# Head norms of the recurrence as two fp32r products on split squares, each step one slot later

## The chip, the core and the metric

The kernel runs on one core of one Trainium2 chip, in one launch. The metric is the device time of that launch in microseconds (us). The core has TensorE (PE: matmuls; its weight loads are shown apart, as PEld), VectorE (DVE), ScalarE (ACT), GpSimd (POOL), and the queues that issue transfers. Each engine works through its own instructions in the order in which they were written; semaphores are the only tie between engines. A wait therefore holds up everything that stands behind the waiting instruction on its engine.

## What is computed

A trunk of two layers on 512 tokens of width 1024. Each layer is a half step of a SwiGLU network, a mixer of three kinds of heads in parallel, a second half step, and a gated embedding:

```
x = x + 0.5 * swiglu(rms_norm(x, ffn1_norm[i]), ...)
x = x + hybrid_mixer(rms_norm(x, mix_norm[i]), i, w_in[i], w_out[i], ...)
x = x + 0.5 * swiglu(rms_norm(x, ffn2_norm[i]), ...)
gate = jax.nn.sigmoid(rms_norm(x, ple_norm[i]) @ ple_w_gate[i])
x = x + gate * rms_norm(p[i] @ ple_w_proj[i], ple_post_norm[i])
```

The mixer projects x once and cuts the result into tiles. Queries and keys of the attention heads, and the output of the recurrence, are normed per head of 64 (or 32) values:

```
q_n = rms_norm(nq.reshape(b, t, NSA_HEADS, HEAD_DIM), nsa_q_norm)
k_s = rms_norm(kvh(sk), nsa_k_norm[1]);  k_w = rms_norm(kvh(wk), nsa_k_norm[2])
k_d = rms_norm(dk.reshape(b, t, DIFF_HEADS, 2, DIFF_QK_DIM), diff_k_norm)
o_h = hgrn2_scan(q_h, i_gate, hi..., log_f)
o_h = rms_norm(o_h, hgrn_out_norm) * jax.nn.silu(hg...)
```

The recurrence (`hgrn2_scan`) is computed as a causal product with decays. The kernel builds its scores level by level, for blocks that double in size.

## The kernel before

Values lie with their features across the 128 partitions and the 512 tokens along the free side. A large product is made from split operands: each fp32 array is kept as a high part rounded to fp32r and an fp32r remainder, and `three` (L531 to L533) issues high by high, low by high and high by low. PE takes an fp32r matmul as one instruction, and an fp32 matmul as two.

**The recurrence** runs between the first projections (`group_c`) and the attention. It has 30 slots: three pairs of heads p, and for each the levels -1 to 8, so slot = 10 p + lev + 1. In what follows level product s is PE's product of slot s. All engines loop over the same slots, each in its own order:

- PE (`hgrn`, L728): the level's score products (L676) into two of the four `side` banks; in slots 10 and 20 also `hgrn_values(p - 1)` (L689, L696), which gathers the output of the pair before; then filler for the dense array: products of the projection of `natA` (slots 0 to 7) or of the tiles nq0, nq1, nq2, sk, wk, dk0, dk1 (`tile_part`, from slot 9 on, two or three of a tile's eight parts in a slot).
- ACT (L1213, L1227, L1230): the exponential of the decays for the level two slots on; in slots p, lev = 7 and 8 it also copies far scores out of the banks (`far_scores`, L1243), for which `hgrn_values` waits; it rounds the weights of the chunk two places on to their high part (`split`, L1048).
- POOL (L497): the two operands `zv` of a level, from ACT's decays, in two buffers.
- DVE: the exponents for the level two slots on (L1816, L1818), then `keep` (L1833 or L1839), which copies the level's scores out of its two banks and so frees them; evacuation of a finished tile (`scaled`, L1716); the low part of a weight chunk (L1580).

**A head norm** is four steps on a [128, 512] tile. ACT squares it into one of two buffers (`head_square`, L1086, `sq`). PE multiplies by a block matrix of ones (`head_squares`, L566), in fp32, into a `side` bank. ACT turns that into the factor with Ln and Exp (`head_factor`, L1097 and L1100), after which the bank is free. DVE multiplies (`normed`, L1736, or for the recurrence's output `out_norm`, L1881). In the recurrence of each layer eight norms are made so: of the pairs 0 and 1 of the recurrence's output, ("hgrn", 0) and ("hgrn", 1), and of nq0, nq1, nq2, sk, wk, dk0. For a tile whose last product part stands in slot t, the square stands in slot t + 1, the ones product at the end of slot t + 2, factor and multiplication in slot t + 3 (`tiles_after`). Six more head norms of a layer, and the compressed keys', stand elsewhere.

The `side` banks are handed out in turn. A level takes two, a ones product one, and the taker waits until the former content of its bank is read.

## Time and profile before

| what | value |
|---|---|
| median of 3 runs | 2235.11 us (2234.0 to 2235.28) |
| the profiled execution | 2234.47 us, of which 2232.7 us are its span from first to last instruction |
| granted TensorE clock | 0.999 of full |
| busy: PE, DVE, ACT, POOL | 2217.7, 1184.8, 916.4, 154.9 us |
| recurrence, layer 0 / layer 1 | from 445 to 555 us / from 1554 to 1664 us of the span |

Times in the rows below count from the start of the span. A row of a timeline is a start, a duration, the engine, the line, the operation, the names out<-in, the shape and how many instructions are merged in it. In brackets stands idle time of the engine just before it and who ended it. A matmul's shown duration reaches beyond the start of the next, since they are pipelined; what a matmul costs is the distance from start to start. The same holds, by some 0.08 us, for DVE and ACT.

### The profile page before, as it was taken

The page shows a single profiled execution, that of the slowest core. Times are in us where ns is not written, and L with a number is a line of the kernel's source. Part 1 is how long each engine was busy: PE and PEld are TensorE (multiplying, and loading weights), DVE is VectorE, ACT ScalarE, POOL GpSimd, SP SyncE. Part 2 cuts the span into 40 slices and gives each one's busy share as a digit, 9 for nine tenths or more (in the row PEclk, how much of TensorE's full clock was granted, in tenths as well). Part 3 has the DMA queues.
Part 4 walks back from the last instruction along what each step waited for, and adds up shares of the span by engine and source line. Part 5 has one row for each costly group of instructions (what it writes and reads, how often), then busy time and mean ns, then how long its engine had stood idle before and what let it go on. Part 6 is the DMA issues. An engine that isn't in the chain of part 4 may idle for free. (4 is left out here: it accounts for less than half of the span.)

```text
span 2232.7 us, 29159 instructions
## 1 busy us (share of the span) xinstructions
PE 2217.7 (99%) x11564; PEld 1755.3 (79%) x11564; DVE 1184.8 (53%) x1934; ACT 916.4 (41%) x1518; POOL 154.9 (7%) x155
## 2 busy tenths in 40 slices
PE   9999999999999999999999999999999999999999
PEld 7888888876667888888888888878766678888887
DVE  6444433577785444433664443346776764444336
ACT  5222223545784322222552222235557752232234
POOL 0000000033111000000000000000431210000000
PEclk9999999999999999999999999999999999999999
DMA  6323334312113323333222333343121132333332
GB/s 207 127 95 103 89 96 143 131 58 77 55 37 90 104 95 97 100 103 100 95 95 95 101 97 91 100 150 117 58 75 48 43 102 95 99 100 101 96 98 83
DMA packets 69280, 214.40 MB, mean 96 GB/s; under 512 B 8175, under 2 KB 15343, under 8 KB 69146
## 3 DMA queue, kind: packets, MB, share of 16 engines
q1 hardware_dynamic: 60452, 191.10, 27.2%
q10 hardware_dynamic: 8694, 21.45, 2.9%
q8 instruction: 92, 1.51, 0.3%
q14 instruction: 42, 0.34, 0.0%
HBM read 208.30 MB, written 5.40 MB: 96 GB/s over the span
## 5 line engine op out<-in xcount | busy, mean ns | idle before, releaser
L531 PE MATMUL main<-xh,wh 128*128 128x512 f32 x1896 | 756.0, 399 | 3.7 <-DVE wl L2130 2.0
L533 PE MATMUL main<-xh,wl 128*128 128x512 f32 x1896 | 740.4, 391 | 0.0
L532 PE MATMUL main<-xl,wh 128*128 128x512 f32 x1896 | 740.4, 390 | 0.0
L1580 DVE TENSOR_TENSOR wl<-raw,wh 128x1024 fp32r<-128x1024 f32 (+2 forms) x336 | 404.3, 1204 | 354.9 <-ACT wh L1048 353.6
L1048 ACT ACTIVATE wh<-raw 128x1024 fp32r<-128x1024 f32 (+1 forms) x370 | 375.4, 1016 | 452.2 <-PE main L533 425.0
L531 PEld LDWEIGHTS main<-xh,wh 128*128 128x128 f32 x1896 | 356.6, 188 | 101.0 <-issue 21.8
L533 PEld LDWEIGHTS main<-xh,wl 128*128 128x128 f32 x1896 | 356.6, 188 | 75.2
L532 PEld LDWEIGHTS main<-xl,wh 128*128 128x128 f32 x1896 | 356.7, 188 | 74.3 <-issue 3.8
L532 PE MATMUL main<-ffl,wh 128*128 128x512 f32 x704 | 274.3, 390 | 0.0
L531 PE MATMUL main<-ffh,wh 128*128 128x512 f32 x704 | 274.3, 390 | 0.0
L533 PE MATMUL main<-ffh,wl 128*128 128x512 f32 x704 | 274.3, 390 | 0.0
L1112 ACT ACTIVATE fg<-fg 128x512 f32<-128x512 f32 x88 | 55.6, 632 | 398.4 <-DVE fg L1672 398.4
L1672 DVE TENSOR_TENSOR fg<-main,rb 128x512 f32<-128x512 f32 x88 | 60.8, 691 | 235.0 <-PE main L533 218.2
L532 PEld LDWEIGHTS main<-ffl,wh 128*128 128x128 f32 x704 | 132.3, 188 | 27.4
L533 PEld LDWEIGHTS main<-ffh,wl 128*128 128x128 f32 x704 | 132.3, 188 | 27.3
L531 PEld LDWEIGHTS main<-ffh,wh 128*128 128x128 f32 x704 | 132.2, 188 | 27.3
L1685 DVE TENSOR_TENSOR fu<-main,rb 128x512 f32<-128x512 f32 x88 | 60.8, 690 | 147.2 <-PE main L533 147.2
L497 POOL TENSOR_TENSOR zv<-ev,hall 128x256 f32<-128x256 f32 x108 | 82.0, 782 | 258.5 <-ACT ev L1213 200.1
L1381 ACT ACTIVATE probs<-probs,small 128x128 f32<-128x128 f32 (+3 forms) x160 | 87.5, 551 | 1.7 <-DVE small L1987 1.7
L506 POOL TENSOR_TENSOR wl<-raw,wh 128x768 fp32r<-128x768 f32 (+1 forms) x34 | 69.0, 2036 | 235.7 <-ACT wh L1048 235.7
L478 POOL MEMSET w2p<- 128x768 f32 x2 | 1.5, 740 | 1153.6 <-PE main L533 1153.6
L1839 DVE COPY_PREDICATED sdiag<-lmask,side 128x512 f32<-128x512 uint32 x84 | 57.1, 733 | 17.0 <-PE side L676 17.0
(262 smaller groups left out, 2082.4 us busy)
## 6 DMA issues: line engine op xcount, KB each, us to landing
raw<-in_ffn_gate SPq DMA_DIRECT2D x87, 512.0 KB, 3.5
raw<-in_ffn_up SPq DMA_DIRECT2D x87, 512.0 KB, 3.4
raw<-in_ffn_down SPq DMA_DIRECT2D x64, 448.0 KB, 3.3
raw<-in_w_in_t SPq DMA_DIRECT2D x40, 512.0 KB, 3.5
raw<-in_ffn_down SPq DMA_DIRECT2D x32, 512.0 KB, 3.6
raw<-in_wout SPq DMA_DIRECT2D x24, 384.0 KB, 3.2
w<-in_cmp_w ACTq DMA_DIRECT2D x16, 512.0 KB, 4.3
raw<-in_ple_gate SPq DMA_DIRECT2D x16, 512.0 KB, 3.3
```

What stands on the lines that cost most here:

```text
L497: nc.gpsimd.tensor_tensor(o.rearrange(cut, two=2, l=size)[:, :, which, :], e.rearrange(cut, two=2, l=size)[:, :, which, :], operand.rearra ...
L506: nc.gpsimd.tensor_tensor(wl[:, c % SLOTS, 0:n], raw[:, c % SLOTS, 0:n], wh[:, c % SLOTS, 0:n], ALU.subtract).then_inc(*tick("weights_lo_p ...
L531: nc.tensor.matmul(out, lh, rh, start=start, stop=False, **kw)
L532: nc.tensor.matmul(out, lh, rl, start=False, stop=False, **kw)
L533: return nc.tensor.matmul(out, ll, rh, start=False, stop=stop, **kw)
L1048: nc.scalar.activation(wh[:, c % SLOTS, 0:n], raw[:, c % SLOTS, 0:n], ACT.Copy).then_inc(*tick("weights_hi", c, layer="all"))
L1112: nc.scalar.activation(fg[:, ft % 2, :], fg[:, ft % 2, :], ACT.Silu).then_inc(*tick("gate_silu", name, ft))
L1381: nc.scalar.activation(pr, pr, ACT.Exp, bias=sm("nm", k), scale=-1.0, accum_out=sm("sum", k)).then_inc(*tick("probs", u, g, i))
L1580: nc.vector.tensor_tensor(wl[:, c % SLOTS, 0:n], raw[:, c % SLOTS, 0:n], wh[:, c % SLOTS, 0:n], ALU.subtract).then_inc(*tick("weights_lo", ...
L1672: nc.vector.tensor_tensor(fg[:, ft % 2, :], bank_of((name + "_gate", ft))[:], rb[:], ALU.mult).then_inc(*tick("gate_scaled", name, ft, fre ...
L1685: nc.vector.tensor_tensor(fu[:, ft % 2, :], bank_of((name + "_up", ft))[:], rb[:], ALU.mult).then_inc(*tick("up_scaled", name, ft, frees=( ...
L1839: ins = V.copy_predicated(out, m, src)
```

## The change

Eight norms of each layer's recurrence are changed, 16 in all. ACT squares the tile twice: in fp32 into `zs[:, 0]`, and rounded to fp32r into `zhi`. DVE subtracts (`square_low`) and writes the fp32r remainder `zlo`. PE multiplies an fp32r copy of the block matrix with `zhi` and then with `zlo`, two one-instruction matmuls instead of a two-instruction one. `zhi`, `zlo` and buffer 0 have no second copy, so a square of such a norm, and the one after it, wait for the ones product of the norm just before. (`zhi` and `zlo` lie where two arrays of the attention or of the network are not in use at the time.)

The steps stand in slots by two tables: the square at `SQUARED_AT`, the subtraction one slot later, the ones product two slots later and now right behind the level's products (and behind `hgrn_values`), ahead of the tile parts; Ln, Exp and the multiplication at `FACTOR_AT`. ACT's Ln and Exp now stand behind `far_scores`, where they stood ahead. The multiplication of a recurrence output moves from lev 1 to lev 2.

```diff
+SQUARED_AT = {("hgrn", 0): 10, "nq0": 12, "nq1": 15, "nq2": 18, ("hgrn", 1): 20, "sk": 22, "wk": 24, "dk0": 27}
+FACTOR_AT = {("hgrn", 0): 13, "nq0": 15, "nq1": 18, "nq2": 21, ("hgrn", 1): 23, "sk": 25, "wk": 27, "dk0": 29}
...
@@ PE, head_squares @@
+                    if name not in SQUARED_AT:
+                        pe.wait_ge(*done("head_sq", name))
+                        nc.tensor.matmul(out[:, 0:n], const_(blocks), zs[:, slot_of(name) % 2, 0:n], start=True,
+                                         stop=True).then_inc(*tick("head_squares", name))
+                        return
+                    pe.wait_ge(*done("blocks_rounded", 1, layer=0))
+                    pe.wait_ge(*done("head_sq_lo", name))
+                    nc.tensor.matmul(out[:], blocks_r[blocks][:], zhi[:], start=True, stop=False)
+                    nc.tensor.matmul(out[:], blocks_r[blocks][:], zlo[:], start=False,
                                      stop=True).then_inc(*tick("head_squares", name))
...
@@ PE, hgrn @@
-                        if p and lev == 0:
-                            head_squares(("hgrn", p - 1), "sum64")
+                        for name in named_at(SQUARED_AT, slot - 2):
+                            head_squares(name, "sum32" if name[0] == "d" else "sum64")
...
-                        for name in tiles_after(slot, 2):
-                            head_squares(name, "sum32" if name[0] == "d" else "sum64")
...
@@ ACT, head_square @@
-                    if k >= 2:
+                    if k >= 1 and (name in SQUARED_AT or norm_order[k - 1] in SQUARED_AT):
+                        act.wait_ge(*done("head_squares", norm_order[k - 1]))
+                    elif k >= 2:
                         act.wait_ge(*done("head_squares", norm_order[k - 2]))
...
+                    if name in SQUARED_AT:
+                        nc.scalar.activation(zs[:, 0, :], operand, ACT.Square).then_inc(*tick("head_sq", name))
+                        nc.scalar.activation(zhi[:], operand, ACT.Square).then_inc(*tick("head_sq_hi", name))
+                        return
...
@@ DVE, hgrn @@
-                            if p and lev == 1:
+                            if p and lev == 2:
                                 out_norm(("hgrn", p - 1), 4 + p, col("hout"), "hgrn_out", p - 1)
...
-                            for name in tiles_after(slot, 3):
-                                normed(name)
+                            for name in named_at(SQUARED_AT, slot - 1):
+                                square_low(name)
+                            for name in named_at(FACTOR_AT, slot):
+                                if name in NORMED:
+                                    normed(name)
...
+                def square_low(name):
+                    dve.wait_ge(*done("head_sq_hi", name))
+                    nc.vector.tensor_tensor(zlo[:], zs[:, 0, :], zhi[:],
+                                            ALU.subtract).then_inc(*tick("head_sq_lo", name))
```

Two copies on DVE in the first network make the fp32r block matrices, once.

PE, slots 13 and 14 (levels 2 and 3 of the second pair of heads). `zv` are a level's operands; L676 becomes L697, L566 becomes L586 and L587, L531 to L533 become L545 to L547. Before:

```order
L676 MATMUL side<-zv 64x64 [waits head_ln,near_scores,decayed]
L676 MATMUL side<-zv 64x64 x15
...
L533 MATMUL main<-xh,wl 128x512
L566 MATMUL side<-sq,const 128x512 [waits head_sq,near_scores]
L676 MATMUL side<-zv 64x64 [waits near_scores,decayed]
L676 MATMUL side<-zv 64x64 x15
L531 MATMUL main<-xh,wh 128x512
```

After, slot 14 and the head of slot 15:

```order
L697 MATMUL side<-zv 64x64 [waits head_ln,near_scores,decayed]
L697 MATMUL side<-zv 64x64 x15
L586 MATMUL side<-zhi,sum_r 128x512 [waits head_sq_lo,blocks_rounded,near_scores]
L587 MATMUL side<-zlo,sum_r 128x512
L545 MATMUL main<-xh,wh 128x512
...
L697 MATMUL side<-zv 64x64 [waits near_scores,decayed]
```

The ones product of nq0 moved from the end of slot 13, ahead of level product 14, to behind it, and it waits for DVE's subtraction instead of ACT's square.

DVE, from `keep` of slot 12 to that of slot 14. Before:

```order
L1839 COPY_PREDICATED sdiag<-lmask,side 128x512 [waits masks_in,near_scores,hgrn_scores] x2
L1881 SCALAR_TENSOR_TENSOR mixed<-main,cols,acc 128x512 [waits head_factor]
L1716 TENSOR_TENSOR z<-main,rb 128x512 [waits product]
L1580 TENSOR_TENSOR wl<-raw,wh 128x1024 [waits weights_hi]
L1816 TENSOR_TENSOR ev<-hall 128x16x16 [waits decayed]
L1818 TENSOR_TENSOR ev<-hall 128x16x16
L1839 COPY_PREDICATED sdiag<-lmask,side 128x512 [waits masks_in,near_scores,hgrn_scores] x2
L1816 TENSOR_TENSOR ev<-hall 128x8x32 [waits decayed]
L1818 TENSOR_TENSOR ev<-hall 128x8x32
L1839 COPY_PREDICATED sdiag<-lmask,side 128x512 [waits masks_in,near_scores,hgrn_scores] x2
```

After, the same stretch:

```order
L1865 COPY_PREDICATED sdiag<-lmask,side 128x512 [waits masks_in,near_scores,hgrn_scores] x2
L1742 TENSOR_TENSOR z<-main,rb 128x512 [waits product]
L1604 TENSOR_TENSOR wl<-raw,wh 128x1024 [waits weights_hi]
L1842 TENSOR_TENSOR ev<-hall 128x16x16 [waits decayed]
L1844 TENSOR_TENSOR ev<-hall 128x16x16
L1865 COPY_PREDICATED sdiag<-lmask,side 128x512 [waits masks_in,near_scores,hgrn_scores] x2
L1916 SCALAR_TENSOR_TENSOR mixed<-main,cols,acc 128x512 [waits head_factor]
L1910 TENSOR_TENSOR zlo<-sq,zhi 128x512 [waits head_sq_hi]
L1842 TENSOR_TENSOR ev<-hall 128x8x32 [waits decayed]
L1844 TENSOR_TENSOR ev<-hall 128x8x32
L1865 COPY_PREDICATED sdiag<-lmask,side 128x512 [waits masks_in,near_scores,hgrn_scores] x2
```

The output norm's multiplication (L1881, now L1916) moved behind the `keep` of slot 13, and the subtraction for nq0 (L1910) stands behind it.

ACT, slot 18 (level 7 of the second pair), from the decay's exponential to that of slot 19. Before:

```order
L1213 ACTIVATE ev<-ev 128x512 [waits exponent]
L1243 ACTIVATE soff<-side 128x128 [waits hgrn_values,hgrn_scores]
...
L1048 ACTIVATE wh<-raw 128x1024 [waits product,raw_full2]
L1086 ACTIVATE sq<-z 128x512 [waits head_squares,scaled]
L1213 ACTIVATE ev<-ev 128x512 [waits exponent]
L1243 ACTIVATE soff<-side 128x256 [waits hgrn_values,hgrn_scores]
```

After:

```order
L1238 ACTIVATE ev<-ev 128x512 [waits exponent]
L1268 ACTIVATE soff<-side 128x128 [waits hgrn_values,hgrn_scores]
...
L1122 ACTIVATE acc<-side,const 128x512 [waits hgrn_out,head_squares]
L1125 ACTIVATE acc<-acc 128x512 [waits head_ln]
L1067 ACTIVATE wh<-raw 128x1024 [waits product,raw_full2]
L1108 ACTIVATE sq<-z 128x512 [waits head_squares,scaled]
L1109 ACTIVATE zhi<-z 128x512
L1238 ACTIVATE ev<-ev 128x512 [waits exponent]
L1268 ACTIVATE soff<-side 128x256 [waits hgrn_values,hgrn_scores]
```

Ln and Exp of nq1 came into slot 18 from slot 17, behind the far scores and ahead of the rounding of the weights, and a second square follows.

## Rows read from the trace of the kernel before

**Rows 1.** The page: busy us, share of the span, instructions of each engine.

```profile
PE 2217.7 (99%) x11564; PEld 1755.3 (79%) x11564; DVE 1184.8 (53%) x1934; ACT 916.4 (41%) x1518; POOL 154.9 (7%) x155
```

**Rows 2.** PE's waits: us in total, times, longest.

```profile
PE side L843 <- ACT soff L1243: 0.7, 1, 0.7
PE side L676 <- DVE sdiag L1839: 0.5, 2, 0.3
```

**Rows 3.** Busy time by engine in one stretch, slots 15 to 17.

```profile
core 0: us, PE busy (x) PEld busy (x) DVE busy (x) ACT busy (x) POOL busy (x), PEclk, DMA share, GB/s
497.61:506.54 8.93, 8.91 (x107) 6.35 (x107) 8.16 (x13) 6.00 (x14) 5.04 (x8) 1.00 0.20 61
```

**Rows 4.** PE's timeline, layer 0, slot 11 and slots 13 to 14.

```profile
484.66 0.69 PE L676 MATMUL side<-zv 64*64 64x64 f32 x32
485.29 1.13 PE L566 MATMUL side<-sq,const 128*128 128x512 f32 x2
...
486.49 0.40 PE L532 MATMUL main<-xl,wh 128*128 128x512 f32 x1
486.72 0.40 PE L533 MATMUL main<-xh,wl 128*128 128x512 f32 x1
...
493.22 0.39 PE L533 MATMUL main<-xh,wl 128*128 128x512 f32 x1
493.45 1.02 PE L566 MATMUL side<-sq,const 128*128 128x512 f32 x2
494.40 0.69 PE L676 MATMUL side<-zv 64*64 64x64 f32 x32
```

**Rows 5.** DVE, a subtraction that writes fp32r: group by form, busy us, mean ns.

```profile
L1678 DVE TENSOR_TENSOR ffl<-fu,ffh 128x512 fp32r<-128x512 f32 x88 | 60.1, 683 | 0.4
```

**Rows 6.** DVE's timeline, slots 12 to 14, 16 and 18.

```profile
489.18 1.38 DVE L1839 COPY_PREDICATED sdiag<-lmask,side 128x512 f32<-128x512 uint32 x2 [1.58 <-PE side L676]
490.45 0.73 DVE L1881 SCALAR_TENSOR_TENSOR mixed<-main,cols,acc 128x512 f32<-128x512 f32 x1
491.10 0.68 DVE L1716 TENSOR_TENSOR z<-main,rb 128x512 f32<-128x512 f32 x1
491.70 1.22 DVE L1580 TENSOR_TENSOR wl<-raw,wh 128x1024 fp32r<-128x1024 f32 x1
492.83 0.42 DVE L1816 TENSOR_TENSOR ev<-hall 128x256 f32<-128x256 f32 x1
...
493.50 1.35 DVE L1839 COPY_PREDICATED sdiag<-lmask,side 128x512 f32<-128x512 uint32 x2
...
498.16 0.78 DVE L1736 SCALAR_TENSOR_TENSOR q<-z,small,rn 128x512 f32<-128x512 f32 x1 [0.67 <-ACT rn L1100]
...
502.80 1.34 DVE L1839 COPY_PREDICATED sdiag<-lmask,side 128x512 f32<-128x512 uint32 x2
...
509.52 1.23 DVE L1580 TENSOR_TENSOR wl<-raw,wh 128x1024 fp32r<-128x1024 f32 x1 [1.71 <-ACT wh L1048]
```

**Rows 7.** PE's timeline: level products 15, 17, 18, then values; 15 of layer 1.

```profile
497.61 0.70 PE L676 MATMUL side<-zv 64*64 64x64 f32 x32 [0.25 <-DVE sdiag L1839]
...
503.66 0.68 PE L676 MATMUL side<-zv 64*64 64x64 f32 x16
506.54 0.72 PE L676 MATMUL side<-zv 64*128 64x128 f32 x8
...
514.04 0.44 PE L689 MATMUL main<-sdiag,hv 128*64 128x128 f32 x4
...
1606.34 0.69 PE L676 MATMUL side<-zv 64*64 64x64 f32 x32 [0.26 <-DVE sdiag L1839]
```

**Rows 8.** ACT's timeline, slots 14 and 19.

```profile
496.26 0.63 ACT L1213 ACTIVATE ev<-ev 128x512 f32<-128x512 f32 x1 [2.01 <-DVE ev L1818]
...
511.99 1.19 ACT L1243 ACTIVATE soff<-side 128x256 f32<-128x256 f32 x4
```

**Rows 9.** One DVE line: duration ns least, median, most.

```profile
L1818 DVE TENSOR_TENSOR ev<-hall x42: 409/417/958, 435.9 to 1644.4; 128x256 f32<-128x256 f32 x42
```

More of the change, by code:

```diff
@@ L61 @@
 SMALL = {}
-for _name, _n in (("gq", 1), ("gdq", 1), ("gsub", 1), ("nlam", 1), ("lam2", 64), ("e", 8),
+for _name, _n in (("gq", 1), ("gdq", 1), ("gsub", 1), ("nlam", 1), ("e", 8),
                   ("max", 3), ("tot", 3), ("rec", 3), ("lb", 6), ("lc", 6), ("li", 6), ("ab", 6), ("rt", 4),
@@ L67 @@
 NSMALL = _at
+SMALL["lam2"] = (SMALL["cmax"][0], 64)
 TILES = ["ck", "cv", "hf0", "hf1", "hf2", "hq0", "hq1", "hq2", "sk", "wk", "nq0", "nq1", "nq2", "dk0", "dk1", "dq0",
@@ L100, with named_at @@
 PARTS, LAST_PART = slot_parts()
+SQUARED_AT = {("hgrn", 0): 10, "nq0": 12, "nq1": 15, "nq2": 18, ("hgrn", 1): 20, "sk": 22, "wk": 24, "dk0": 27}
+FACTOR_AT = {("hgrn", 0): 13, "nq0": 15, "nq1": 18, "nq2": 21, ("hgrn", 1): 23, "sk": 25, "wk": 27, "dk0": 29}
+def named_at(places, slot):
+    return [name for name in places if places[name] == slot]
 def tiles_after(slot, distance):
@@ L253, in layers @@
         sq = sb("sq", [P, 2, SEQ])
+        sq_at = place["at"] - 4 * 2 * SEQ
+        zlo = nc.alloc_sbuf_tensor_at("zlo", [P, SEQ], F32R, offset=sq_at)
+        zhi = nc.alloc_sbuf_tensor_at("zhi", [P, SEQ], F32R, offset=sq_at + 4 * SEQ)
+        blocks_r = {name: sb(name + "_r", [P, P], F32R) for name in ("sum64", "sum32")}
         region = place["at"]
@@ L564, in head_squares @@
                     out = take(("head_squares", name), which)
-                    pe.wait_ge(*done("head_sq", name))
-                    nc.tensor.matmul(out[:, 0:n], const_(blocks), zs[:, slot_of(name) % 2, 0:n], start=True,
+                    if name not in SQUARED_AT:
[7 more added lines that the diff above has]
+                    nc.tensor.matmul(out[:], blocks_r[blocks][:], zlo[:], start=False,
                                      stop=True).then_inc(*tick("head_squares", name))
@@ L1283, in hgrn @@
                                     split(CHUNK[(name,)] + AHEAD)
-                            for name in tiles_after(slot, 1):
-                                act.wait_ge(*done("scaled", name))
-                                head_square(name, zt(name))
+                            for name in named_at(SQUARED_AT, slot):
+                                if name in NORMED:
+                                    act.wait_ge(*done("scaled", name))
+                                    head_square(name, zt(name))
                             if (p, lev) == (2, 1):
@@ L1620, in small_exponents @@
                                         ALU.add).then_inc(*tick("fold"))
+                        for n, name in enumerate(("sum64", "sum32")):
+                            V.tensor_copy(blocks_r[name][:], const_(name)).then_inc(*tick("blocks_rounded", n))
                     dve.wait_ge(params_in[counts.layer], 32)
```

7 lines of the change are left out of this document (3 added, 4 removed).

## The prediction

> **What bounds the kernel now.** The page first: PE is busy 2217.7 us of a span of 2232.7 [rows 1], so what makes PE's queue shorter is a gain unless it makes PE wait. Then PE's own waits: in the recurrence they are few and short, 0.25 us in each layer for DVE's `keep` before level product 15, and 0.67 us in layer 0 for ACT's far scores before the first attention scores [rows 2, 7]. Then the stretches, for how close the others are. In slots 15 to 17 DVE is busy 8.16 us of 8.93 [rows 3]. DVE has half of the whole span free [rows 1], but hardly a tenth here, in the place where the change gives it more to do. Last the timelines of PE, DVE and ACT over slots 11 to 19, on which the sum rests. Layer 1 repeats layer 0 some 1108.7 us later (level product 15 at 497.61 and 1606.34, with the same wait [rows 7]), so I work out layer 0 and take it twice, but for the 0.67, which only layer 0 has.
>
> **What is removed on PE.** An fp32 ones product occupies PE for 0.95 us from its start to the next level product (493.45 to 494.40), or 0.86 us where an fp32r product follows: the first ones product starts at 485.29, the second instruction of the following triple at 486.49, and that is 0.34 after the triple's first [rows 4]. (0.34 is what a triple's first takes behind fp32 work; the further ones take 0.23, 486.49 to 486.72.) The two fp32r matmuls that replace it take 0.23 each and inherit the 0.34 of the change of type from the tile part behind them: 0.46 more in the queue. The gain is 0.86 - 0.46 = 0.40 us for each norm, 8 x 0.40 = 3.2 a layer. With the two old waits, if they go (0.25 and 0.67), and some 0.2 of gaps around the old instructions, that is 4.3 us in layer 0.
>
> **What is added.** On ACT a second square of 0.6 us, on DVE a subtraction. The nearest row of that form, two fp32 operands in SBUF and an fp32r result, takes 683 ns [rows 5], about 0.60 from start to start. ACT's is hidden in most slots. DVE's is what PE now waits for, and PE's queue is short of slack towards it: the ones product stands one slot after the subtraction, right behind the level product, and all of PE's work of the slot stands behind it. The two rounded copies of the ones matrices are 128x128 and in the first network, where DVE waits for PE most of the time: nothing.
>
> **The walk, slots 12 to 14.** Level product 12 comes 0.86 earlier, since the ones product of slot 11 is gone, and so does the `keep` that waits for it: 488.32 instead of 489.18 [rows 6]. Then in DVE's new order, by start-to-start distances of the same rows: keep 1.27, tile evacuation 0.60, weights 1.13, exponents 0.67, keep 1.24, which ends at 493.23. Here stands the multiplication for ("hgrn", 0), which needs ACT's decay, Ln and Exp. In slot 14 of before these three took from 496.26 until DVE went on at 498.16, 1.90 [rows 6, 8]. In the new slot 13 they start when the exponents are there, at 492.12, so DVE idles until 494.03. Then 0.65 for the multiplication and 0.65 for the subtraction of nq0: `zlo` is there at 495.36. PE meanwhile: level product 14 stood at 494.40; less 0.86 and 0.95, plus 0.46, it could start at 493.1. Its bank wants the Ln of ("hgrn", 0), done at 493.3: 0.2 lost. It is through at 494.0, and the ones product waits until 495.4: 1.4 lost. **Slot 14 costs 1.6 us**, and level product 15 starts at 498.1, half a microsecond later than before.
>
> **Slot 17.** Before, the `keep` of slot 16 ran from 502.80 [rows 6], when PE was almost at level product 17 (503.66 [rows 7]): DVE is a slot behind. In the new order it has two subtractions more in front of or behind that `keep`, the multiplication of nq0 ahead of it, and the head start of 0.86. I get 504.8 for the `zlo` of nq1, PE through level product 17 at 503.8: **1.0 lost**. Level product 18 starts at 507.6 instead of 506.54.
>
> **Slots 18 to 20.** ACT's far scores of slot 19, for which `hgrn_values(1)` waits, started at 511.99 [rows 8], last in a chain: far scores of slot 18, rounded weights (ACT), their low part (DVE, at 509.52 after idling 1.71 for ACT [rows 6]), exponents (DVE), decay (ACT). Before, that ended 0.9 ahead of the values at 514.04 [rows 7]. Now Ln and Exp of nq1 stand inside it (0.70 + 0.54), then the multiplication of nq1 ahead of the exponents (0.73), and the chain starts 0.5 later with level product 18. So the far scores end at 515.7 and PE is there at 514.2: **1.5 lost**.
>
> **Slots 20 to 29**, counted from the end of the values, since DVE's `keep` of slot 20 waits for them. Up to the subtraction of ("hgrn", 1) DVE has keep, exponents, keep (which waits for level product 21, 3.3 after the values' end), evacuation, weights and subtraction: ready at 7.1 after. PE, with the ones product of nq2, the three parts of sk, level product 21, three parts of wk and level product 22, gets there at 5.5: **1.6 lost**. sk, wk and dk0 find their `zlo` ready. But level product 25 wants the `keep` of slot 24, which stands behind DVE's scores of the compressed keys (**0.5**), and level product 26 wants the Ln of sk, behind ACT's second square of wk (**0.65**). The far scores of slot 29, now ahead of dk0's Ln and Exp, come early enough for the first attention scores. DVE enters the attention some 3.5 late, PE 2.5; I take no further stall there, since DVE has waits for PE in its first logits.
>
> Sum of a layer: 1.6 + 1.0 + 1.5 + 1.6 + 0.5 + 0.65 = 6.85 lost, 4.3 gained: +2.5 in layer 0, and without the 0.67 +3.2 in layer 1: +5.7. The 2234.47 of the profiled execution (2232.7 of span and 1.8 around it) become 2240.2. The median of the runs stands 0.64 above the profiled one: **2240.8 us**.
>
> **A rule of the Trainium skill against the change.** One exponent instruction of DVE took 958 ns at most where the median of its line is 417 [rows 9]. The skill ("SBUF — State Buffer", "SBUF: two separate sides") says that GpSimd and a DVE instruction with two SBUF inputs take one pair of ports in turn, whole instruction by whole instruction; the trace's 958 fits it, since that line reads two SBUF operands too. The subtraction has two such inputs. What this would do is a rival of its own, priced from the same row.
>
> **Rivals.**
> - *The cover holds* (faster). DVE and ACT keep up, no ones product waits. For it: ACT is busy 6.00 of 8.93, and the table gives every step a slot. Against it: rows 3 and the idle 0.67 at 498.16, which shows DVE bound by ACT's latency. It gives 2235.1 - 4.3 - 3.6 = 2227.2. Chance 0.13.
> - *Half of it* (same). The ones products wait, but the two chains that I carried furthest, values(1) and the pair of level products 25 and 26, come out even: 2 x (1.5 + 1.15) = 5.3 less, 2235.5. The error of a walk grows with its length, and DVE may catch up by some 1 us in its idle times (1.71 at 509.52). Chance 0.26.
> - *The walk* (slower by 0.25%). It needs no mishap, only the orders and durations of before. Chance 0.46, own range 2238 to 2243.5.
> - *Ports* (slower). Each subtraction in the path (nq0, nq1, ("hgrn", 1)) meets POOL and takes 0.54 more (958 - 417), six in two layers, 3.2: 2244.0. It decides from the first of them that overlaps a product of POOL. Chance 0.12.
> - *The two fp32r matmuls cost what the fp32 one did*: then 2 x 3.2 more, 2247.2. Against it is every triple in rows 4. Chance 0.03.
>
> **Numbers.** Likeliest 2240.8. The low end leaves out the cover that holds, the high end takes in the ports with an error of 2: 2231 to 2246. A measurement of this kernel tells about 0.2% (4.5 us) from no change. Faster than 2230.6: 0.15, the cover and a little of the second. Above 2239.6: some 0.33 of the walk's 0.46 and the last two (0.15): 0.48. Between: 0.37.
>
> **What would show it.** Right: in the new profile the ones product (L586) waits for DVE's `zlo`, over 1 us, in slots 14, 17 and 22 of both layers, and L710 (values) waits for `soff` in slot 20; the level products of slots 15 and 18 start some 0.5 and 1 us later than 497.61 and 506.54. A norm's two fp32r matmuls take 0.46. Wrong: if `zlo` of nq0 is ready by 494.0, the first term falls, and with it the sum, since all later ones start from there.

## The result, and the profile after

| | before | after |
|---|---|---|
| median (range, runs) | 2235.12 us (2233.84 to 2235.28, 6) | 2251.57 us (2250.66 to 2252.49, 6) |
| the profiled span | 2232.7 us | 2250.7 us |

The ratio of the times is 1.0075 (95% interval 1.0065 to 1.0086): slower by 0.75%. The prediction had the sign, slower, but its 2240.8 is 10.8 us short and its range ended at 2246.

PE is busy for as long as in [rows 1], and the span is 18.0 longer. That the two busy times are equal is chance: the cheaper products shorten PE's work, and a lower clock, further down, lengthens it again (in the first experiment, where the clock stays up, PE is busy 2213.3 us). From the page of after, the busy line:

```profile
PE 2217.7 (99%) x11564; PEld 1758.0 (78%) x11564; DVE 1200.0 (53%) x1952; ACT 924.7 (41%) x1534; POOL 158.3 (7%) x155
```

PE's waits of after, over the whole span (us in total, times, longest). Where [rows 2] had 1.2 us in three waits, the lines of the recurrence now hold 19.5:

```profile
PE side L586 <- DVE zlo L1910: 13.8, 8, 2.8
PE main L710 <- ACT soff L1268: 2.9, 2, 1.5
PE side L697 <- DVE sdiag L1865: 1.8, 4, 0.6
...
PE side L697 <- ACT rn L1122: 1.0, 2, 0.5
```

Now PE's timeline of after in layer 0, at the places of [rows 7] and of the prediction's steps (start, duration, line, operands; in brackets the idle time ahead and who ended it):

```profile
495.57 0.47 PE L586 MATMUL side<-zhi,sum_r 128*128 128x512 f32 x1 [1.35 <-DVE zlo L1910]
...
498.27 0.69 PE L697 MATMUL side<-zv 64*64 64x64 f32 x32
...
505.81 0.47 PE L586 MATMUL side<-zhi,sum_r 128*128 128x512 f32 x1 [1.75 <-DVE zlo L1910]
...
508.52 0.72 PE L697 MATMUL side<-zv 64*128 64x128 f32 x8
...
516.73 0.44 PE L710 MATMUL main<-sdiag,hv 128*64 128x128 f32 x4 [1.47 <-ACT soff L1268]
...
526.33 0.47 PE L586 MATMUL side<-zhi,sum_r 128*128 128x512 f32 x1 [1.64 <-DVE zlo L1910]
...
549.21 1.14 PE L697 MATMUL side<-zv 64*128 64x256 f32 x8
552.88 0.76 PE L586 MATMUL side<-zhi,sum_r 128*128 128x512 f32 x1 [2.54 <-DVE zlo L1910]
...
555.28 1.65 PE L862 MATMUL side<-kk,q 64*128 64x128 f32 x8
...
559.46 0.92 PE L862 MATMUL side<-kk,q 64*128 64x384 f32 x4
```

The same two places in the trace of before (level product 29, second attention scores), and the wait for the subtraction of dk0 in layer 1 of after:

```profile
545.33 1.14 PE L676 MATMUL side<-zv 64*128 64x256 f32 x8
...
550.47 0.92 PE L843 MATMUL side<-kk,q 64*128 64x384 f32 x4
```

```profile
1671.35 0.47 PE L586 MATMUL side<-zhi,sum_r 128*128 128x512 f32 x1 [2.83 <-DVE zlo L1910]
```

The waits of slots 14, 17, 20 and 22 are those of the prediction, that of slot 17 longer. The one at 552.88, for the subtraction of dk0 in slot 29, is not: there the prediction had none. Level product 29 stood at 545.33 before, so 549.21 is 3.9 late; the second attention scores stood at 550.47, so 559.46 is 9.0 late. More is lost in the ten microseconds after level product 29 than in the eighteen slots ahead of it. Layer 1 adds 9.1 in the same way.

What holds DVE there, from its timeline of after (its line L1762 is the multiplication of a norm, L2002 the three small products of the compressed keys) and POOL's:

```profile
546.76 0.68 DVE L1742 TENSOR_TENSOR z<-main,rb 128x512 f32<-128x512 f32 x1
547.35 2.63 DVE L1762 SCALAR_TENSOR_TENSOR kk<-z,cols,acc 128x512 f32<-128x512 f32 x1
549.90 2.83 DVE L1910 TENSOR_TENSOR zlo<-sq,zhi 128x512 fp32r<-128x512 f32 x1
...
553.97 0.34 DVE L2002 TENSOR_TENSOR small<-small,gates 128x8 f32<-128x8 f32 x3
```

```profile
547.04 5.15 POOL L520 TENSOR_TENSOR wl<-raw,wh 128x1024 fp32r<-128x1024 f32 x2
```

The two DVE instructions, 0.75 and 0.68 us elsewhere, take 5.38 us together, about as long as GpSimd's two products beside them (5.15). In both kernels GpSimd starts these products right behind level product 28. In the kernel before, DVE was a slot further on by then: it had the multiplication behind it and no subtraction to do, and it was the three tiny instructions of 8 elements that took 3.20 us, with nobody waiting for them. From the trace of before, POOL and DVE:

```profile
542.30 4.71 POOL L506 TENSOR_TENSOR wl<-raw,wh 128x1024 fp32r<-128x1024 f32 x2
```

```profile
542.61 0.94 DVE L1962 TENSOR_REDUCE small<-cp 128x24 f32<-128x768 f32 x1
...
543.92 3.20 DVE L1967 TENSOR_TENSOR small<-small,gates 128x8 f32<-128x8 f32 x3
```

And what follows the stall: busy time and granted clock (PEclk) of after, in stretches around it and, last, in layer 1 behind the wait for the subtraction of nq0.

```profile
core 0: us, PE busy (x) PEld busy (x) DVE busy (x) ACT busy (x) POOL busy (x), PEclk, DMA share, GB/s
550.34:552.88 2.54, 0.01 (x1) 0.03 (x1) 2.54 (x2) 1.21 (x4) 1.85 (x1) 0.88 0.66 206
552.88:554.00 1.12, 1.12 (x3) 0.93 (x4) 1.05 (x3) 0.00 (x0) 0.00 (x0) 0.50 0.72 172
...
558.00:559.00 1.00, 1.00 (x4) 0.81 (x3) 0.28 (x2) 0.00 (x0) 0.00 (x0) 0.50 0.00 0
559.00:560.00 1.00, 1.00 (x6) 0.37 (x5) 0.00 (x0) 0.00 (x0) 0.00 (x0) 0.95 0.00 0
...
1614.00:1615.00 1.00, 1.00 (x3) 0.76 (x3) 1.00 (x3) 0.46 (x1) 0.47 (x1) 0.50 0.00 0
```

PE is granted 1.2 GHz instead of 2.4 for some 6.8 us at the stall of layer 0 (the last 0.6 us of the stall are among them), for 3.4 us behind that of layer 1, and for 3.4 us from 1613.8 on. At the lower clock the fp32r matmuls of a triple follow each other in 0.43 us instead of 0.23. In the trace of before the clock is at its full level from the 13th microsecond to the last three.

**The account.** The fp32 product of dk0 stood ahead of level product 29; its two fp32r matmuls, 0.46 us, now stand behind it. In layer 0, 3.9 to level product 29, these 0.46, 2.54 of stall, less the old wait of 0.67: 6.2. The second scores are 9.0 late, so the low clock took 2.8. In layer 1 level product 29 is 4.3 late (0.5 of it low clock, by the first experiment, where that layer has 3.8), then 0.46, 2.83 of stall and 1.6 of low clock: 9.1. So of some 18.1, the orders took 3.9 + 3.8 + 2 x 0.46 - 0.67 = 7.9, where the prediction had 5.7; the two stalls took 5.4 and the low clock 4.9, where it had nothing. The first experiment, with neither stall nor low clock, confirms the split: its second scores of layer 0 are 4.7 earlier than in after, which is 2.54 less a new wait of 0.60, and 2.8.

### The profile page after: what moved, and what is told of

Its sections match the earlier page's. It is cut to its first block and busy times, and to the rows that moved or that the text cites. A ratio compares the mean times of both kernels' runs of the same rounds, so it can differ in the third digit from the quotient of the medians.

```text
span 2250.7 us, 29195 instructions
## 1 busy us (share of the span) xinstructions
PE 2217.7 (99%) x11564; PEld 1758.0 (78%) x11564; DVE 1200.0 (53%) x1952; ACT 924.7 (41%) x1534; POOL 158.3 (7%) x155
## 5 line engine op out<-in xcount | busy, mean ns | idle before, releaser
L545 PE MATMUL main<-xh,wh 128*128 128x512 f32 x1896 | 753.9, 398 | 3.3 <-DVE wl L2165 1.6
L547 PE MATMUL main<-xh,wl 128*128 128x512 f32 x1896 | 740.6, 391 | 0.0
L545 PEld LDWEIGHTS main<-xh,wh 128*128 128x128 f32 x1896 | 357.0, 188 | 100.1 <-issue 20.5
L547 PEld LDWEIGHTS main<-xh,wl 128*128 128x128 f32 x1896 | 357.2, 188 | 76.0
L545 PE MATMUL main<-ffh,wh 128*128 128x512 f32 x704 | 273.9, 389 | 0.0
L547 PE MATMUL main<-ffh,wl 128*128 128x512 f32 x704 | 273.9, 389 | 0.0
L547 PEld LDWEIGHTS main<-ffh,wl 128*128 128x128 f32 x704 | 132.1, 188 | 27.6
L545 PEld LDWEIGHTS main<-ffh,wh 128*128 128x128 f32 x704 | 132.1, 188 | 27.3
```

Of the source, the lines that this page charges most:

```text
L545: nc.tensor.matmul(out, lh, rh, start=start, stop=False, **kw)
L547: return nc.tensor.matmul(out, ll, rh, start=False, stop=stop, **kw)
```

## Experiments

Times are medians. Those of the kernel before, which ran beside them, are 2234.68 for the first four, 2235.18 for the next four and 2234.78 for the last four; the differences below are to these. Starts of two traces are compared after taking off by how much they differ at slot 11, ahead of the change's first step (up to 1.3 us, from the start of the launch).

### GpSimd's product held back

```diff
 if own == layer and key in ON_GPSIMD:
     n = chunk_width(key)
+    if key == (GROUP_OF["B"][0],):
+        pool.wait_ge(*done("head_sq_lo", "dk0"))
```

> The changed kernel with one added wait: GpSimd's first product of the recurrence (the weights' first low half for the attention, 547.04 for 5.15 us in the trace of after) starts only when the subtraction of dk0 is done. Theory A (the missed term is slot 29: DVE's kk and subtraction of dk0 take 2.63 and 2.83 us beside that product, the ones product of dk0 waits 2.54 us, and the idle PE then gets the lower clock for some 7 us): kk and the subtraction take about 0.7 us each, the wait before the ones product of dk0 falls below 0.3 us, the granted clock behind it stays near 1.00, and the first attention scores start 4.5 to 5.5 us earlier in each layer: 2240 to 2243 us, close to the predicted walk. Rival B (the wait at slot 29 only uses up slack that is lost later anyway, since the attention's weights now come later from GpSimd): the wait goes, but a new one stands before the first attention tiles, and the time stays at 2249 to 2252. Rival C (the lower clock has another cause than the idle): the wait goes but the clock still falls: about 2246.

2243.24 us (2242.49 to 2243.76, 6 runs), 8.6 over before and 8 under after. DVE's and PE's timelines of this kernel, in layer 0:

```profile
548.02 0.74 DVE L1764 SCALAR_TENSOR_TENSOR kk<-z,cols,acc 128x512 f32<-128x512 f32 x1
549.32 0.69 DVE L1912 TENSOR_TENSOR zlo<-sq,zhi 128x512 fp32r<-128x512 f32 x1 [0.56 <-ACT zhi L1111]
```

```profile
550.95 0.50 PE L588 MATMUL side<-zhi,sum_r 128*128 128x512 f32 x1
...
552.98 0.93 PE L864 MATMUL side<-kk,q 64*128 64x128 f32 x8 [0.60 <-ACT rn L1124]
```

Both instructions are back at their length, the ones product of dk0 doesn't wait, and the clock behind it stays at 1.00. The first attention scores are 3.0 us earlier than in after in layer 0 and 4.0 in layer 1, where 4.5 to 5.5 was expected; the second ones, behind all of the low clock, are 4.7 and 4.9 earlier. **Theory A stands**, B and C fall for the larger part. The time is just above the expected range. Layer 0 has a new wait of 0.60: the attention scores want the bank that Ln of dk0 reads. So a little of B is in it. The waits of the other slots are what they were, but for one: that of nq1 in layer 1 is 1.75 here too, where after had 0.68. There the low stretch ahead of it delays level product 15 by 1.6 us, and DVE catches up meanwhile: of the 1.6 the shorter wait gives 1.1 back. GpSimd's product, pushed back, now stretches L2004, the three small products, to 3.61 us, again with nobody waiting.

### dk0 as before

The edit takes dk0 out of both tables and gives it the old steps:

```diff
+OLD_AT = {"dk0": 27}
 for name, ks in PARTS.get(slot, {}).items():
     tile_part(name, ks)
+for name in named_at(OLD_AT, slot - 1):
+    head_squares(name, "sum32" if name[0] == "d" else "sum64")
...
```

> The changed kernel with the last of the eight norms, dk0, as it was before: one square, one fp32 ones product at the end of slot 28, no subtraction. The other seven are as in the changed kernel. Theory A (slot 29 alone makes 5 to 6 us a layer): no wait of 2.5 us before a ones product in slot 29, no lower clock behind it, 0.4 us a layer lost on the fp32 product: 2240 to 2243 us. Rival B (kk, which GpSimd stretches too, delays the attention whatever the norm does): the gain is under 3 us, 2248 or more. Both earlier waits (ones products of slots 14, 17, 22, about 4.7 us a layer) stay.

2244.46 us (2243.93 to 2244.56, 4 runs), 9.8 over before. `kk` still takes 2.62 us beside GpSimd's product, but PE's next wait is the old one, 0.67 us for the far scores ([rows 2]), and the clock stays high. A stretched instruction costs only if PE waits for it: B falls. The time is 1.5 above the range of A. It is 1.2 slower than the first experiment: 0.4 for each of the two fp32 products is expected, and the rest is in their spread.

### TensorE doesn't wait for the subtraction

```diff
-pe.wait_ge(*done("head_sq_lo", name))
+pe.wait_ge(*done("head_sq_hi", name))
-nc.tensor.matmul(out[:], blocks_r[blocks][:], zlo[:], start=False,
+nc.tensor.matmul(out[:], blocks_r[blocks][:], zhi[:], start=False,
...
 act.wait_ge(*done("head_squares", norm_order[k - 1]))
+if norm_order[k - 1] in SQUARED_AT:
+    act.wait_ge(*done("head_sq_lo", norm_order[k - 1]))
```

> The changed kernel, but both fp32r matmuls of a norm read the rounded square, so TensorE doesn't wait for DVE's subtraction (the remainder is left out of the sum and the rounded square counted twice: the computation is changed). The subtraction is still done by DVE in its place, and ACT's next square waits for it too. Theory A (what costs is TensorE's wait for the subtraction): the waits of L586 (13.8 us in eight instructions in after) are nearly gone, the values' wait for the far scores stays in part, 2230 to 2238 us. Rival D (the added work on DVE and ACT costs through the other chains, the keep and far scores that come late, and the waits only move from the ones products to the level products): the waits of L586 go, but those for sdiag, rn and soff grow by as much, over 2243 us.

2241.76 us (2240.57 to 2242.14, 7 runs), 7.1 over before, between what the two theories expected. PE's waits of this kernel decide between them:

```profile
PE side L697 <- DVE sdiag L1867: 6.4, 8, 1.0
PE main L710 <- ACT soff L1270: 2.9, 2, 1.5
...
PE side L697 <- ACT rn L1124: 1.0, 2, 0.5
```

The 13.8 us before the ones products are gone, and the waits for `keep` (sdiag) have grown from 1.8 to 6.4. (ACT's added wait for the subtraction shows nowhere in this profile.) Of the 4.7 us of waits for `zlo` in slots 14, 17 and 22 of layer 0 little comes back: the values of slot 20 stand 1.1 us earlier than in after, level product 29 stands 1.2 earlier. Three quarters of what this trace gains over that of after are gained behind level product 29, and the first experiment has those without touching the other waits. **Theory A falls for slots 14 to 26, D holds there**: the waits for `zlo` are where DVE's lateness shows; take them away, and it shows one instruction later, at the level product.

### The fp32r pair alone, in the old slots

`PAIRED` are the eight norms, and `zr` are two fp32r buffers in the place of the two of `sq`.

```diff
-nc.scalar.activation(zs[:, k % 2, 0:n], operand, ACT.Square)
+to = zr[:, k % 2, :] if name in PAIRED else zs[:, k % 2, 0:n]
+nc.scalar.activation(to, operand, ACT.Square)
...
+if name in PAIRED:
+    half = zr[:, slot_of(name) % 2, :]
+    nc.tensor.matmul(out[:], blocks_r[blocks][:], half, start=True, stop=False)
+    nc.tensor.matmul(out[:], blocks_r[blocks][:], half, start=False, stop=True)
```

> The kernel before with two fp32r matmuls on a once rounded square in place of the fp32 ones product of the same eight norms, in the old slots, with no subtraction and no second square (the computation is changed: the remainder is left out and the rounded square counted twice). It measures the gain on TensorE by itself. By the prediction's term, 0.40 us for each of 16 norms: 2228 to 2230 us. Rival E (the pair costs what the fp32 product did): 2235. If the old waits go too (0.67 and 0.25), up to 1.2 us less.

2232.47 us (2232.04 to 2234.74, 10 runs), 2.2 under before (ratio 0.9990, interval 0.9981 to 1.0000). PE's timeline of this kernel in slot 11, to be laid beside [rows 4]:

```profile
485.03 0.50 PE L573 MATMUL side<-zr,sum_r 128*128 128x512 f32 x1
485.36 0.39 PE L574 MATMUL side<-zr,sum_r 128*128 128x512 f32 x1
485.59 0.39 PE L535 MATMUL main<-xh,wh 128*128 128x512 f32 x1
485.82 0.40 PE L536 MATMUL main<-xl,wh 128*128 128x512 f32 x1
```

From the ones product to the triple's second instruction it is 0.79 us, where [rows 4] have 1.20: 0.41 for one norm, the prediction's 0.40. But 16 of them bring 2.2 us and not 6.4. Of the missing 4.2, 2.0 stand in PE's keep waits (0.5 in [rows 2]), and some 0.8 in a gap ahead of the ones product of wk, of 0.6 in each layer, which the profile puts down to no other engine (in before it was under 0.2). The rest lies in gaps too short for this list:

```profile
PE side L687 <- DVE sdiag L1853: 2.5, 8, 0.4
...
PE side L573 <- issue: 1.1, 2, 0.6
```

**Even with nothing added on ACT or DVE the gain is a third of what the products give up.** Before, PE arrived at several level products just as DVE's `keep` freed their bank; there a faster PE only arrives early. The expected 2228 to 2230 is missed by 2.5 us.

### The move alone

One square, fp32 ones products, no subtraction, but all steps in the slots of the changed kernel:

```diff
-if name not in SQUARED_AT:
+if True:
     pe.wait_ge(*done("head_sq", name))
...
-for name in named_at(SQUARED_AT, slot - 1):
-    square_low(name)
```

> The norms' steps in the slots of the changed kernel (ones product right behind the level product two slots after the square, Ln, Exp and multiplication one slot later, far scores ahead of them), but with the fp32 ones products, one square and no subtraction of the kernel before: the move by itself. Theory S (DVE's added subtractions make the chains late, the slots are harmless): 2232 to 2237, no wait of the values for soff. Theory M (the slots themselves cost: Ln, Exp and the multiplication of nq1 now stand inside the chain that ends in the far scores of slot 19): the values wait again 1 to 1.5 us for soff in each layer, keep waits stay, 2237 to 2241.

2238.2 us (2236.56 to 2239.18, 10 runs), 3.0 over before (ratio 1.0014, interval 1.0005 to 1.0023). Its PE waits:

```profile
PE main L710 <- ACT soff L1268: 2.9, 2, 1.5
PE side L581 <- DVE sdiag L1865: 1.0, 2, 0.5
```

**Theory M holds**: the slots cost 3.0 us by themselves, and the values' wait for the far scores is there in its full 1.5 with no subtraction anywhere.

### The pair in the new slots

The same kernel, with the pair on top of it:

```diff
-to = zs[:, k % 2, 0:n]
+to = zr[:, k % 2, :] if name in SQUARED_AT else zs[:, k % 2, 0:n]
...
+nc.tensor.matmul(out[:], blocks_r[blocks][:], half, start=True, stop=False)
+nc.tensor.matmul(out[:], blocks_r[blocks][:], half, start=False, stop=True)
```

> As the run before it in this call, but with two fp32r matmuls on the once rounded square of each of the eight norms (computation changed: the remainder is left out, the rounded square counted twice): the shorter work on TensorE in the new slots. In the old slots the same exchange gave 2.2 us instead of the predicted 6.4, because TensorE then waited for DVE's keep. Theory S: 2230 to 2234, as in the old slots. Theory M: no better than the moved fp32 version by more than 2 us, 2236 to 2240.

2236.54 us (2234.75 to 2238.13, 10 runs), 1.4 over before, 1.7 under the moved fp32 version. As in the old slots, the shorter products bring only part of 6.4, here about a quarter. It is inside M's range, and no more than 2 us better, as M had it.

### Both squares, no subtraction

```diff
-for name in named_at(SQUARED_AT, slot - 1):
-    square_low(name)
```

and the two matmuls read `zhi`.

> The changed kernel without DVE's subtraction, ACT's two squares and all slots as they are, both matmuls on the rounded square (computation changed: the remainder is left out). Against the version whose subtraction stays and isn't waited for (2241.8) it tells what DVE's eight subtractions a layer cost by themselves. Theory S: 4 to 8 us of those 2241.8 go, 2234 to 2238. Theory M: under 3 us go, 2239 to 2242. Rival A2 (ACT's second square delays the chains): it differs from the once squared version by over 2 us.

2237.57 us (2237.03 to 2238.78, 10 runs), 2.4 over before. ACT's second square costs 1.0 us (to the version ahead of it), so rival A2 falls. The subtraction costs 7.1 - 2.4 = **4.7 us** even where PE doesn't wait for it, inside what S expected. Level by level in layer 0, the version with the unawaited subtraction loses 0.6 us against this one at level product 16, 0.5 at level product 19 and 0.6 at level product 23, behind the subtractions of nq0, nq1 and ("hgrn", 1), and 0.1 or nothing behind the other five: 1.9 a layer, so the two traces hold 3.7 of the 4.7 that the medians give. Three subtractions of some 0.6 us go straight into the time. For nq1, [rows 3] show why, with DVE busy 8.16 us of 8.93; for the other two, DVE's timeline of the version with the unawaited subtraction has no idle time from the subtraction to the `keep` that PE waits for.

### The split with the move undone

```diff
-FACTOR_AT = {("hgrn", 0): 13, "nq0": 15, "nq1": 18, "nq2": 21, ("hgrn", 1): 23, "sk": 25, "wk": 27, "dk0": 29}
+FACTOR_AT = {("hgrn", 0): 12, "nq0": 14, "nq1": 17, "nq2": 20, ("hgrn", 1): 22, "sk": 24, "wk": 26, "dk0": 29}
...
-for name in named_at(SQUARED_AT, slot - 2):
-    head_squares(name, "sum32" if name[0] == "d" else "sum64")
...
 for name, ks in PARTS.get(slot, {}).items():
     tile_part(name, ks)
+for name in named_at(SQUARED_AT, slot - 1):
+    head_squares(name, "sum32" if name[0] == "d" else "sum64")
...
-if p and lev == 2:
+if p and lev == 1:
     out_norm(("hgrn", p - 1), 4 + p, col("hout"), "hgrn_out", p - 1)
```

> The changed kernel with the move undone and the split kept: the ones product of a norm at the end of the slot after its square's (that of (hgrn, 0/1) too), Ln, Exp and multiplication in the slots of the kernel before, the subtraction where the changed kernel has it; dk0 keeps its late factor. Theory M (the move costs): 2238 to 2244, better than the 2251.6 of the changed kernel by the values' wait and by part of the keep waits. Theory S (the subtraction on DVE costs, and TensorE needs it earlier here): waits before the ones products of 1.5 us or more in slots 13, 16 and 22, 2250 or more.

2261.97 us (2256.8 to 2263.51, 4 runs), 26.8 over before. PE's line for the ones products:

```profile
PE side L586 <- DVE zlo L1910: 21.1, 11, 3.3
```

Here S is right, and further out than I had it: the split needs the move. Without it PE waits 21.1 us for subtractions: in layer 0 2.13 us in slot 13, 1.22 in slot 16, 3.33 in slot 21 and 2.66 in slot 25 (expected were 1.5 or more in slots 13, 16 and 22). Around three of these waits, that of slot 25 in layer 0 and those of slots 21 and 25 in layer 1, the clock is at 1.2 GHz again, for 3.4, 6.8 and 6.8 us. The change's two halves belong together; the move costs 3.0 and spares far more.

### An idle time of TensorE put into the kernel before

```diff
+if (u, part) == (0, 0):
+    pe.wait_ge(*done("probe"))
...
+dve.wait_ge(*done("cmp_probs"))
+for n in range(3):
+    i = V.tensor_reduce(sm("csum", 0, 24), flat, AX.X, ALU.add)
+    i.then_inc(*(tick("probe") if n == 2 else tick("probing", n)))
```

> The kernel before, in which DVE repeats its last reduction of the compressed keys three times at the end of the recurrence and TensorE's first attention scores wait for the third: an idle time of TensorE of some 2.9 us (from 548.0 to 550.9 in layer 0) at the place where the changed kernel waits, with nothing of the change in it. Theory I (the idle time itself brings the lower clock): the granted clock falls to about 0.5 for 4 us or more behind it, and the time rises by more than twice the idle: 2 x (2.9 + 2 to 3) = 10 to 12 us, 2245 to 2247. Rival C (the clock in after fell for another reason): the clock stays at 1.00 and the time rises by the idle alone, 2240.5 to 2241.5.

2245.37 us (2244.84 to 2245.96, 4 runs), 10.6 over before. Layer 0, windows and PE's timeline:

```profile
547.25:550.96 3.71, 0.00 (x0) 0.00 (x1) 3.61 (x5) 0.52 (x2) 0.00 (x0) 1.00 0.42 150
550.96:552.00 1.04, 1.04 (x9) 0.71 (x10) 0.60 (x1) 0.00 (x0) 0.00 (x0) 0.96 0.00 0
552.00:553.00 1.00, 1.00 (x3) 0.81 (x4) 0.96 (x7) 0.00 (x0) 0.00 (x0) 0.50 0.00 0
```

```profile
550.96 0.93 PE L845 MATMUL side<-kk,q 64*128 64x128 f32 x8 [3.71 <-DVE small L1977]
...
554.61 1.25 PE L845 MATMUL side<-kk,q 64*128 64x384 f32 x4
```

The idle is 3.71 us, of which 0.67 stood there before, so the first scores come 3.1 late. Then the granted clock is 0.50 for 3.4 us and the lateness grows to 4.6. Layer 1 repeats it: 3.98 us idle, 3.4 at 0.50, which costs 1.5 to 1.6. **Theory I holds**: an idle PE is enough to bring the lower clock, with nothing of the change in the kernel. The low stretch cost 1.5 us here and 2.8 in layer 0 of after, where it lasted twice as long.

The same with one reduction:

```diff
-for n in range(3):
+for n in range(1):
```

> The same with one reduction more, so an idle time of TensorE of some 1.0 us at the same place. By all runs so far idle times of 1.0 to 1.8 us in the recurrence are followed by a granted clock of 1.00. Theory I: no lower clock, the time rises by the idle alone, 2 us: 2237. If even this lowers the clock there: 2239 to 2242.

2238.87 us (2237.52 to 2242.08, 10 runs), 4.1 over before. In the profiled execution the idle times are 1.78 in layer 0 and 2.04 in layer 1, and the clock stays at 1.00 behind both. The first scores come 1.2 late in layer 0 and a further 2.2 in layer 1, where before had no wait: 3.4. I had reckoned 2 with an idle of 1.0; DVE does the reduction later than I thought, and 0.7 of the 4.1 is not placed. Nor is it shown that the clock stays up in every execution: the profiled one has a mean granted clock of 1.000, four of the other nine have 0.998, and two of these four took some 3 us more than the median; where the clock fell in them can't be told. And the sentence of this expectation on all runs so far is not right: in layer 1 of after a wait of 1.35 us was followed by the low clock from 1613.8 on.

### The far scores ahead of the decay

On top of the first experiment, in slot 19:

```diff
+if (p, lev) == (1, 8):
+    far_scores(p, lev)
 if lev >= 0 and g + 2 < 3 * LEVELS:
     decay(g + 2)
```

> The changed kernel with GpSimd's product held back as in the first experiment (2243.2), and in slot 19 ACT makes the far scores before the decay of that slot, not behind it. Nothing in the far scores needs that decay; only ACT's order ties them to Ln and Exp of nq1, the weights and the exponents. Theory M (that order makes the values wait 1.5 us a layer once the slots are moved): the wait of L710's line for soff goes and 2 to 3 us with it, 2240 to 2241.5. Rival K (DVE's keep of slot 20, exponents and evacuations behind it are what sets slots 20 to 26, so the gain is lost there): 2242.5 to 2243.5.

2240.29 us (2239.73 to 2242.98, 10 runs), 2.95 less than the first experiment. (The profiled execution is the slowest of the ten.) L710 has no wait left, and the values and every level product behind them in layer 0 are 1.5 us earlier. **Theory M holds, K falls**: this chain was pure order on ACT, and what is saved there is kept to the end.

### Five norms split, three as before

```diff
-SQUARED_AT = {("hgrn", 0): 10, "nq0": 12, "nq1": 15, "nq2": 18, ("hgrn", 1): 20, "sk": 22, "wk": 24, "dk0": 27}
+SQUARED_AT = {("hgrn", 0): 10, "nq2": 18, ("hgrn", 1): 20, "sk": 22, "wk": 24}
+OLD_AT = {"nq0": 12, "nq1": 15, "dk0": 27}
...
```

The steps of the three stand where they stood before, and the far scores as in the experiment ahead of this one.

> A better version, if there is one: nq0, nq1 and dk0 as in the kernel before (fp32 product, old slots), the other five norms as in the changed kernel, and the far scores of slot 19 before the decay. The subtractions of nq0 and nq1, which cost 0.6 us each, Ln and Exp of nq1 in the chain to the values, and the stall of slot 29 are gone. By terms: 5 x 0.41 gained a layer, 0.6 lost for the subtraction of (hgrn, 1), 0.5 to 1.2 for level products 25 and 26, so 0.3 to 1 us a layer gained: 2233 to 2235. If DVE's keep eats the shorter products here too, as it did where the remainder was left out: 2236 to 2238. By no theory does it beat the kernel before by over 0.2%.

2236.13 us (2234.99 to 2237.2, 10 runs), 1.4 over before; ratio 1.0006 (interval 0.9997 to 1.0016). That is the range in which DVE's `keep` eats the shorter products. The best split version that was tried doesn't differ from the kernel before by more than 0.2%. PE still waits 1.7 us in each layer for the subtraction of ("hgrn", 1), and 1.0 for `keep` and `rn` at level products 25 and 26.

## Why the prediction was wrong

Step by step, in its own terms.

**The price of the product: right.** 0.40 predicted, 0.41 measured. **Eight times that as the gain: wrong as a gain, though not in the sum.** The pair alone gives 1.1 a layer, not 3.2. The walk has DVE's times in it and takes the difference back in its losses; but the 2227.2 of the rival *The cover holds* was never to be had. With nothing added anywhere the pair reaches 2232.5, and this rival's price was wrong by 5 us.

**Slot 14: right.** `zlo` of nq0 predicted at 495.36, there at 495.4; the wait 1.35 for 1.4; level product 15 at 498.27 for 498.1. The 0.2 for Ln of ("hgrn", 0) was 0.38 for `keep`.

**Slot 17: mis-sized.** 1.0 predicted, 1.75 measured (also in layer 1 of the first experiment), and level product 18 at 508.52 for 507.6. PE was at its place nearly as foreseen, but `zlo` was ready at 505.7, not 504.8. From DVE's timeline of after:

```profile
497.79 0.96 DVE L1844 TENSOR_TENSOR ev<-hall 128x256 f32<-128x256 f32 x1
...
501.63 1.23 DVE L1604 TENSOR_TENSOR wl<-raw,wh 128x1024 fp32r<-128x1024 f32 x1 [0.68 <-ACT wh L1067]
...
504.66 1.00 DVE L1910 TENSOR_TENSOR zlo<-sq,zhi 128x512 fp32r<-128x512 f32 x1
```

The subtraction was stretched beside GpSimd (1.00 for 0.68), and DVE idled 0.68 for the rounded weights of ACT, which now stand behind Ln and Exp of nq0; the two make up the 0.9. (The exponent's 0.96 stood in the trace of before too.) The 0.75 in each layer is two thirds of the gap between the 5.7 of the prediction's orders and the 7.9 measured. The rest is gain that didn't come: PE's waits in layer 0 add up to 7.6 us up to level product 26, and by the account the orders made that layer 3.7 late, so 3.9 were gained and not 4.3.

**Slot 20: right**, 1.47 for 1.5, and by the chain that was named: the move alone has this wait, and reordering ACT removes it. **Slot 22: right**, 1.64 for 1.6. **Level products 25 and 26: right**, 0.55 (`keep`) and 0.48 (`rn`) for 0.5 and 0.65. What is not right is the reading of slots 14, 17 and 22 as a wait that the ones product causes: the third experiment shows that DVE is late there whether or not the ones product waits, and the seventh that its added time is the cause.

**Slot 29: the step that failed.** The prediction says "sk, wk and dk0 find their `zlo` ready" and "I take no further stall there". For sk and wk it holds; dk0 waited 2.54 and 2.83 us. Without these two waits and the low clock (first experiment) the kernel is 8.6 us over before, where the likeliest value, 2240.8, was 5.7 over and the end of the range, 2246, some 11. The walk was not carried through slots 27 to 29, where GpSimd turns from its products of about 0.8 us to the weights' low halves of 2.6. The rival *Ports* named the mechanism and put it at the wrong places and at the wrong size: its 0.54 was taken from the longest exponent in [rows 9], which had met one of the short products. The row that held the price was in the same trace, the 3.20 us of three instructions of 8 elements. The first experiment shows the mechanism: with the product moved away, 2.63 and 2.83 become 0.74 and 0.69. The rule of the Trainium skill ("SBUF — State Buffer", "SBUF: two separate sides"), that the pair is taken for a whole instruction, is what the trace agrees with: the stretch is as long as GpSimd's instruction, not a share of DVE's.

**The clock: not in the prediction.** It read the granted clock as a constant, since it was one in the recurrence of before, and 4.9 of the 18.0 us came from there. The first probe shows that an idle time brings it without the change, the second that a shorter one can pass without it.

**What is left open.** Behind the wait of nq0 in layer 1 (1.35 us, with 0.32 shortly ahead of it) the clock fell in after and in the version with the far scores ahead, and not in the first two experiments, with the same waits; behind that of layer 0 it fell in none of these. In the version with the move undone, PE waited 3.33 us in slot 21 of either layer, and the clock fell in layer 1 alone. Nor do the runs tell why the low stretch of layer 0 in after lasted 6.8 us and its others 3.4. The median of after, 16.5 above before, is 1.5 less than the 18.0 of the two spans. The profiled execution has the lowest mean granted clock of the six (0.996; the others 0.997 to 0.999) and with one other the longest span (2250.7; the others 2248.8 to 2250.7). So the low clock seems to have taken less in the others than the 4.9 us of the account; where it fell in them can't be told, since its stretch at the start of the launch differs too (3.4 us in before, 6.8 in the version with the far scores ahead, none in the second experiment).

Two corrections to what stands ahead of the prediction. It says that semaphores are the only tie between engines; the 2.63 and 2.83 us above are a second tie, between DVE and GpSimd, with no semaphore in it. And in the section on the change, the place given for `zhi` and `zlo` is wrong: `zlo` lies over buffer 0 of `sq`, the fp32 square itself, and `zhi` is buffer 1.

## What to carry to other kernels

- A cheaper instruction on the bound engine is worth only what its partners let through. Before adding work to pay for it, take the work out alone: here that shows 2.2 us of 6.4.
- When a change delays one engine, follow it to the first point where another engine's long instructions begin, and price the meeting by the longest row that has met them, even if nobody waited for it there.
- A stall of PE can have a second price, the clock behind it. Where two engines' orders only just cover each other, look for steps that an order ties together without any data between them, as the far scores and the decay of slot 19.

## What was unexpected of the hardware

- Three DVE instructions of 8 elements take 3.20 us beside GpSimd's two products of 128x1024 and 0.34 us without them; 512-element ones go from 0.68 to 2.83. The reduction with a single input, 128x768, took 0.94 us beside the same two products, and 0.94 without them.
- After 1.78 and 2.04 us of idle PE ahead of the attention the granted clock stayed at 1.00; after 3.71 and 2.54 it went to 0.50, for 3.4 and 6.8 us, and cost 1.5 and 2.8 us. After a wait of 3.33 us in slot 21 of the version with the move undone it stayed at 1.00 in layer 0 and fell in layer 1, so the length of the idle time doesn't settle it alone.
